# Moving product 4 forward and the next blocks' high part back in the seven-product jobs of a two-layer streaming encoder

## The reference

```
x += 1/2 * SwiGLU_a(RMSNorm(x))          # 1024 -> 2 x 2816 -> 1024
x += mixer(RMSNorm(x))                   # layer 0: retention, layer 1: stick-breaking attention
x += 1/2 * SwiGLU_b(RMSNorm(x))
x += sigmoid(RMSNorm(x) @ W_gate) * (p[i] @ W_proj)
```

## Time and profile before

| | |
|---|---|
| median of three runs | 2784.55 us |
| the profiled execution's own time | 2784.26 us |
| its span | 2782.7 us |
| TensorE matmul busy | 2744.7 us, 99% |
| TensorE weight load busy | 2699.7 us, 97% |
| VectorE busy | 1920.1 us, 69% |
| ScalarE busy | 1207.2 us, 43% |
| mean granted TensorE clock | 0.996 of full speed |
| matmuls of line L618 (the seven products) in the chain of waits | 42% of the span |

### The profile page before, as it was taken

The page is one execution under the profiler, slowest core; times in us unless marked ns, Lnnn a source line. Parts: engine busy times, 40 slices in busy tenths (PEclk is TensorE's granted clock), DMA queues, the critical chain, the costliest instruction groups (busy, mean ns, idle before and its releaser), DMA issues.

```text
span 2782.7 us, 47474 instructions
## 1 busy us (share of the span) xinstructions
PE 2744.7 (99%) x18946; PEld 2699.7 (97%) x18946; DVE 1920.1 (69%) x2691; ACT 1207.2 (43%) x1629; POOL 191.7 (7%) x190
## 2 busy tenths in 40 slices
PE   8999999999999999999999999999999999999997
PEld 8999999999999999999999999999999999999997
DVE  7888864646464678888557788865555568888755
ACT  5445443323132444454444455444534443545443
POOL 0000003101010110000010000002000020000021
PEclk9999999999999999999999999999999999999998
DMA  3322323333232313323321222223222112232231
GB/s 120 95 84 79 97 79 124 110 103 114 92 110 95 104 55 94 87 81 92 93 76 60 85 85 87 88 84 121 88 83 91 68 61 72 77 101 77 86 99 53
DMA packets 80909, 246.96 MB, mean 89 GB/s; under 512 B 8465, under 2 KB 25121, under 8 KB 79681
## 3 DMA queue, kind: packets, MB, share of 16 engines
q1 hardware_dynamic: 71408, 204.67, 23.6%
q0 software_dynamic: 9296, 39.40, 3.9%
HBM read 226.74 MB, written 17.30 MB: 88 GB/s over the span
## 4 chain that ended last, share of the span: by engine, by line
PE 97%; DVE 2%; ACT 0%; issue 0%; DMA 0%; ACTq 0%; SPq 0%; DVEq 0%
PE ps L618 42%; PE ps L547 35%; PE ps L930 7%; PE ps L806 4%; PE ps L983 2%; PE ps L599 1%; PE ps L904 1%; PE ps L1017 1%; PE ps L967 1%; PE ps L871 1%; PE ps L855 0%; PE ps L1003 0%; PE ps L874 0%; PE ps L849 0%; PE ps L883 0%
## 5 line engine op out<-in xcount | busy, mean ns | idle before, releaser
L1086 ACT ACTIVATE w_hi<-raw 128x1024 fp32r<-128x1024 f32 (+2 forms) x210 | 201.3, 959 | 522.4 <-PE ps L547 382.3
L1729 DVE TENSOR_TENSOR w_lo<-raw,w_hi 128x1024 fp32r<-128x1024 f32 (+2 forms) x210 | 238.1, 1134 | 100.5 <-ACT w_hi L1086 97.5
L547 PE MATMUL ps<-x_hi,w_hi 128*128 128x320 f32 x1216 | 283.7, 315 | 9.7 <-DVE x_lo L1734 8.7
L547 PE MATMUL ps<-x_hi,w_lo 128*128 128x320 f32 x1216 | 277.6, 310 | 0.0
L547 PE MATMUL ps<-x_lo,w_hi 128*128 128x320 f32 x1216 | 277.4, 309 | 0.0
L547 PEld LDWEIGHTS ps<-x_hi,w_hi 128*128 128x128 f32 x1216 | 204.3, 188 | 13.5 <-DVE w_lo L2472 8.7
L547 PEld LDWEIGHTS ps<-x_lo,w_hi 128*128 128x128 f32 x1216 | 203.9, 188 | 0.0
L547 PEld LDWEIGHTS ps<-x_hi,w_lo 128*128 128x128 f32 x1216 | 203.7, 188 | 0.0
L1150 ACT ACTIVATE wx_hi<-raw 128x1024 fp32r<-128x1024 f32 (+1 forms) x92 | 92.4, 1004 | 252.4 <-PE ps L618 215.1
L618 PE MATMUL ps<-x_hi,w_hi 128*128 128x320 f32 x576 | 178.7, 310 | 0.0
L618 PE MATMUL ps<-x_hi,w_lo 128*128 128x320 f32 x576 | 177.9, 309 | 0.0
(11 more groups left out here) (310 smaller groups left out, 7714.4 us busy)
## 6 DMA issues: line engine op xcount, KB each, us to landing
raw<-wst SPq DMA_DIRECT2D x292, 512.0 KB, 3.6
raw<-wst SPq DMA_DIRECT2D x96, 384.0 KB, 3.2
raw<-wst SPq DMA_DIRECT2D x32, 256.0 KB, 2.6
s<-st_d POOLq DMA_DIRECT2D x8, 1024.0 KB, 5.1
sts_o<-s POOLq DMA_DIRECT2D x16, 512.0 KB, 3.3
rd<-dec_d POOLq DMA_DIRECT2D x8, 640.0 KB, 5.5
kc<-kc_d POOLq DMA_DIRECT2D x8, 512.0 KB, 4.3
vc<-vc_d POOLq DMA_DIRECT2D x8, 512.0 KB, 5.2
```

The source lines that it names most:

```text
L547: last = nc.tensor.matmul(out[:, h, :], a, b[:, HALF * h:HALF * (h + 1)], start=start and q == 0, stop=stop and q == 2, skip_group_check=True)
L1086: nc.scalar.activation(w_hi[:, (c["n"] + m) % 2, 0:cols], raw[:, r, 0:cols], ACT.Copy).then_inc(s_whi, 1)
L1729: tt(w_lo[:, p, 0:cols], raw[:, r, 0:cols], w_hi[:, p, 0:cols].bitcast(F), ALU.subtract).then_inc(s_wlo, 1)
```

## The change

It touches the three queues of the seven-product jobs, outside the first down job's own branches. On TensorE product 4 of the job in front goes directly behind its product 3. On ScalarE `silu`, `hi34` and `ghi` go first, then `snap2`, then `hi12` of the next job (in a down job `hi12`, then `snap2`). On VectorE `c12` goes between `s2` and `s3`, the gating and the sums of g follow, and `lo12` and `s4` come behind them; in a job behind a down job `c21` of that job goes ahead of the next blocks' sums.

```diff
@@ TensorE
                             third(old)
-                            second().then_inc(s_prod[2], 1)
-                            sixth().then_inc(s_prod[6], 1)
                             if after_start:
                                 split_up_to("T4")
                             fourth(old)
+                            second().then_inc(s_prod[2], 1)
+                            sixth().then_inc(s_prod[6], 1)
                             fifth()
@@ ScalarE
-                        elif new:
-                            hi12(new)
-                        if made and made["seven"]:
+                        if made:
                             silu(made)
-                            snap2(d)
-                        elif old:
-                            snap2(d)
-                            if made:
-                                silu(made)
                         hi34(d)
                         if made:
                             ghi(made)
+                        if old:
+                            if d["kind"] == "gu":
+                                snap2(d)
+                            if new:
+                                hi12(new)
+                            if d["kind"] == "dn":
+                                snap2(d)
@@ VectorE
                         if summed:
                             c11_c12(summed)
-                            s1_s2(new)
-                            s3(new)
                             c21(summed)
-                            lo12(new)
-                            s4(new)
+                            if new:
+                                s1_s2(new)
+                                s3(new)
+                                lo12(new)
+                                s4(new)
                             lo34(d)
                             continue
                         if new:
                             s1_s2(new)
+                        if made:
+                            c12(made)
+                        if new:
                             s3(new)
+                        if made:
+                            gated(made, 1)
+                            if made["seven"] and made["odd"]:
+                                g_sum(made, 1)
+                            gated(made, 0)
+                            if made["seven"]:
+                                g_sum(made, 2)
+                        if new:
                             if old:
                                 lo12(new)
                             else:
                                 lo1(new)
                                 lo2(new)
-                        if made:
-                            c12(made)
-                            gated(made, 1)
-                            if made["seven"] and made["odd"]:
-                                g_sum(made, 1)
-                        if new and made and made["seven"]:
-                            s4(new)
-                        if made:
-                            gated(made, 0)
-                            if made["seven"]:
-                                g_sum(made, 2)
-                        if new and not (made and made["seven"]):
                             s4(new)
                         lo34(d)
```

## The result

The changed kernel takes 2831.56 us (median of four runs, 2831.18 to 2832.23); the kernel before, run beside it, 2784.05 us (2782.79 to 2785.0). The ratio is 1.0172, with a 95% interval of 1.016 to 1.0184: 47.5 us slower. The prediction was 2828 in a range of 2805 to 2850.

What follows compares the result with a forecast made beforehand. TensorE was taken to bound the kernel, with 97% of the chain of waits. Each piece loses 0.1 + 2 x 1.68 + 2 x 0.55 + 0.93 = 5.5 us; eight make 44, so 2784.3 + 44 = 2828 us, range 2805 to 2850.

Steps and rivals of the forecast that it cites:

- TensorE had nothing to give: Seven-product stages: unbroken TensorE work except 0.59 us before product 7 of the first down job, eight times, 4.7 us.
- The odd job: Job whose finished predecessor (made) is odd: stops before product 7 and the next product 1, 1.68 us lost each.
- the landing: Weight blocks loaded behind VectorE's lo34: first sum taken 3.75 us after lo34 ends, range 3.65 to 4.34.
- The even job: Job with even made predecessor: product 4 waits 0.45 us for c22, plus 0.1 at product 3, 0.55 us lost.
- the end of a piece: Behind the last even job, the down job's product 3 waits for lo34: 0.93 us, besides the even job's 0.55.
- The second job: Second gate and up job of a piece: starts in good order, loses 0 to 0.2 us, taken as 0.1.
- The third piece and the down jobs: Jobs without sums of g: the copy for product 7 and low part come in time, so nothing is lost.
- Half of it: Rival on the weight loads: blocks land before VectorE asks, 16 us less loss, 2812 us; chance 0.12.
- Not slower: Rival on VectorE and ScalarE: their room absorbs the wait, 2784.3 - 4.7 to 2784.3, say 2783 us; chance 0.09.
- The clock: Rival: TensorE's clock falls behind each odd job's stop, 16 x 1.5 = 24 us more, 2852 us; chance 0.07.

Runs made afterwards that it cites:

- both moves: Changed kernel with ScalarE's copies of g behind the copy for product 7 and next high part, and VectorE's lo34 ahead of lo12: 2784.33 us, ratio 1.0002.
- shorter loads: Changed kernel with gate and up slots of the last three pieces loaded by half, 256 KB instead of 512 KB: 2814.6 us, ratio 1.0107.
- the copies of g behind: Changed kernel with ScalarE's copies of g moved behind the copy for product 7 and the next blocks' high part: 2790.59 us, ratio 1.002.
- moving lo34 alone: Changed kernel with VectorE's lo34 moved ahead of lo12 and s4 of the next blocks: 2784.51 us, ratio 1.0003.
- only the copy for product 7 ahead: Changed kernel with only the copy for product 7 moved ahead of ScalarE's copies of g, the high part staying behind them: 2834.58 us, ratio 1.0182.

## Why the prediction was right, step by step

*TensorE had nothing to give.* Right: with all waits cut (both moves) the time is that of before. The stop named as 0.59 us was mis-sized: it is counted from the end of the last matmul, and the next could have started before that end; 8 x 0.40 = 3.2 us were to be had, not 4.7.

*The odd job.* Right step by step. Counted from 235.26 (237.21 - 1.95) the profiled job has its first sum at 5.28 (5.51 predicted), c12 at 6.62 (6.85), the copies of g at 9.49 and 10.40 (9.72, 10.63), the copy for product 7 at 11.03 (11.26), the high part at 11.35 (11.63), the low part at 12.43 (12.72), lo34 at 14.30 (14.58), and the next job starts at 13.82 (14.00). Its lo34 in front ended at 1.54 and not 1.76, which moves all of it. The mean odd job lost 1.80 and not 1.68, because the landing isn't 3.75 each time: from the end of lo34 to the first sum it is 3.90 in the mean of the 16 and 3.55 to 4.82, and a job lasts that distance and another 10.1 to 10.2 us, 13.79 to 15.05. Landings that VectorE had absorbed are now on the path; one slow transfer even shows in a third piece, 4.87 us, and cost 0.7 us there.

*The even job* and *the end of a piece*: 0.55 and 0.55 + 0.93 forecast, 0.55 and 1.63 measured; six of the eight ends lost 1.52, the other two 1.88 and 2.00. *The second job*: 0.1 forecast, 0.40 in piece 1 and 0.07 in piece 2. In piece 1 it doesn't start in good order: the lo34 ahead of it ends 1.66 us into it, before the change too, where it ends at 1.18 in piece 2, so its landing comes later. With the copies of g behind it is back at the 12.40 of before; moving lo34 alone doesn't help it.

*The third piece and the down jobs*: nothing forecast; down jobs unchanged at 9.24, third pieces +1.1 us in all.

*The rivals.* Half of it: shorter loads do give 17 us, so the price of the landing was near (16), but in the change the landing stays last. Not slower: its point was a low part that begins by 11.1; it began at 12.43.

The clock: granted 1.00 through all the stops that the change made, the longest of 2.0 us; the warning of the Trainium skill, "TensorE: Matmul & The Clock Gate" (section "A second HAM failure mode: psum-queue depth-cycling"), isn't borne out by these stops. But stops of that size don't always leave the clock alone. In the run with only the copy for product 7 ahead it fell once, behind a stop of 1.98 us before a product 1, to a mix of 2.4 and 1.2 GHz:

```profile
2452.00:2457.00 5.00, 5.00 (x25) 5.00 (x24) 5.00 (x7) 0.77 (x2) 0.00 (x0) 0.66 0.23 79
```

And the prediction's reading that the kernel before shows such a fall only behind its stop of 2.92 us missed others, one of them in the second layer's mixer. The first row is that kernel just behind a wait of 0.95 us, the second the changed kernel around the same wait:

```profile
2248.00:2252.00 4.00, 4.00 (x14) 1.45 (x16) 0.58 (x2) 0.54 (x2) 0.00 (x0) 0.57 0.44 135
```

```profile
2285.00:2290.00 5.00, 4.64 (x29) 3.06 (x30) 1.57 (x4) 1.15 (x3) 0.00 (x0) 1.00 0.31 108
```

The same wait went both ways; the fall cost the kernel before an estimated 0.43 x 4 = 1.7 us. So the length of a stop, on which the prediction relied, doesn't settle it: a fall costs about what the prediction put on it (1.5 us), and the reason given against this rival was not enough.

The occupancy view of "Perfetto Trace Analysis" in the Trainium skill (section "Identifying the Most-Contended Engine") would not have seen the loss coming: VectorE is at 69% before and 68% after.

The median is 3.5 us above the forecast. The odd jobs were 1.9 us too short in it, the second jobs 1.1, the ends 1.2, and the third pieces, put at nothing, 1.1: 5.3 in all. The fall of the clock that the changed kernel was spared takes back about 1.7; that the total came this near is luck to that extent, while the large terms came near one by one.

## What to carry to other kernels

When operations are reordered across two in-order queues, follow the dependences around until they come back to where they began, and compare that loop with the period of the engine that bounds; busy shares say nothing about it. A stop of the bounding engine names only the link that came last: removing the one at product 7 moved it to product 1. Shorten the loop instead; here a shorter landing gave back 17 of 47.5 us, the copies of g moved out of it 41, and one subtraction moved into a hole of it nearly all.

## What the runs showed that I had not expected

TensorE's order alone, with queues that suited the old one, costs 39 us, and the new queues with the old order 131 us, while the whole change costs 47.5: the parts don't add up, since each order is only right for the other. And VectorE's wait ahead of the low part is no measure of a loss: 2.50 us of it in an odd job of the change went with 1.8 us lost, while with lo34 moved ahead 1.4 to 1.8 us in these places cost nothing, nor did 2.55 us in a job of the third piece.
